# Every second transfer of expert weights begun from ScalarE's queue

## The chip, the cores and the metric

The kernel runs on 1 core of one Trainium2 chip. The metric is the device time of one execution, in microseconds (us).

## The reference

One sequence of 512 tokens, model width 1024, float32, passes through two blocks. The first mixes a gated linear attention with a gated convolution and adds a gated embedding; the second mixes an mLSTM branch with a differential attention and ends in an expert layer. Only that layer is touched by the change:

```python
def expert_choice_ffn(h, w_router, w_gate, w_up, w_down):
    cap = EC_CAPACITY * S // N_EXPERTS            # 2 * 512 // 16 = 64 tokens for an expert
    aff = jax.nn.softmax(jnp.einsum('bsd,de->bse', h, w_router), axis=-1)
    g, idx = lax.top_k(aff.transpose(0, 2, 1), cap)
    xe = h[bidx, idx]
    hid = (jax.nn.silu(jnp.einsum('becd,edf->becf', xe, w_gate))
           * jnp.einsum('becd,edf->becf', xe, w_up))
    ye = jnp.einsum('becf,efd->becd', hid, w_down) * g[..., None]
    return jnp.zeros_like(h).at[bidx, idx].add(ye)
```

There are 16 experts of width 2048. `w_gate` and `w_up` are 1024 x 2048 for each and `w_down` is 2048 x 1024: 24 MB of weights for an expert, 384 MB in all, each read once.

## The kernel before

The dense part comes first (up to about 1,109 us into the span): 168 tiles of weights of 512 KB each go through six slots. Then tokens are routed, and the expert loop runs (from 1,140 us to 2,077 us), with a short final norm and the store behind it.

**Chunks and the ring.** An expert's weights come as `PER = 24` chunks of 1 MB: n = 0 to 7 are gate rows, 8 to 15 up rows, 16 to 23 down rows. Chunks are numbered on over all experts, g = 24e + n, from 0 to 383. A ring of `RING = 18` slots holds them: 12 in the tensor `ring_a`, 6 in `ring_b`, chunk g in slot g mod 18. A gate or up chunk is one row of 8 KB for each of the 128 partitions; a down chunk is two rows of 4 KB for each.

**Who loads.** SyncE (SP) begins every transfer of weights, in order of g. The first 18 chunks are fetched while the dense part and the routing run, as their places become free. From g = 18 on, `load_expert` (L603 to L610) waits until the count `s_used` has reached g - 17, that is, until TensorE has finished chunk g - 18, and issues the transfer. A transfer adds 16 to the semaphore of its slot when it has landed.

**TensorE (PE)** works one expert after the other, in an order written out by hand: gate chunk 0; `placed` (L2085), the 8 products that put the previous expert's output back to the tokens; gate 1 to 7 and up 0 to 7 (`gate_up`, L2102); `gather` for the next expert (L2063); `hidden_turned` (L2122) and `gather_turned` (L2070); down 0 to 5 (`down`, L2113); `place_turned` (L2080); down 6 and 7. Each chunk begins with a wait for its slot's semaphore, and its last product adds 1 to `s_used`. In the last expert a product of the residual (L2126) stands behind each down chunk but the last.

**ScalarE (ACT)** runs, for each expert: wait for `used(e, 7)` (gate chunk 7 done); two Silu activations of the gate result (L1076); `gathered(e + 1)`, a copy of the gathered tokens (L1070); the copy `hidT0` (L1080); the copy `place` after `place_turned` (L1082); wait for `used(e, 23)`; the copy `ye` of the expert's output (L1086), for which `placed(e)` waits. It begins no transfer here; its only three are small ones at the very start.

**VectorE** multiplies the two halves of the hidden layer, scales the gathered tokens and adds the placed results; GpSimd does nothing in this loop.

Of the kernel before, what the change touches and what calls it, by code (L numbers as in the profile page):

```python
# [34 lines left out]
NE, CAP, FF = 16, 64, 2048  # L35
BIG = 3.0e38
KB = 1024
RING, RING_A = 18, 12
PER = 24
# [117 lines left out]
STREAM, TILES = dense_stream()  # L157
AT = {(gr.name, gr.i): gr.g for gr in STREAM}
FIRST = [min(gr.g for gr in STREAM if n in gr.tiles) for n in range(len(TILES))]
# [67 lines left out]
def kernel_program(nc, xT_in, pT_in, table, gla_mask_in, rstm_in, negm_in, selr_in, m01_in, dist_in, tiles_in,  # L227
                   w_gk2, diff_lam_2, w_router_2, w_gate_e_2, w_up_e_2, w_down_e_2, norm_f_g_2, x3_store, out):
    ctx = ExitStack()
    with ctx:  # L230
# [10 lines left out]
        def sem(name):  # L241
            return ctx.enter_context(nc.semaphore(name))
# [286 lines left out]
        s_ring = [sem(f"ring_in{s}") for s in range(RING)]  # L529
        s_used = sem("ring_used")  # L530
# [27 lines left out]
        gate_v = w_gate_e_2[0].rearrange("e (k p) f -> p e k f", p=P)  # L558
        up_v = w_up_e_2[0].rearrange("e (k p) f -> p e k f", p=P)
        down_v = w_down_e_2[0].rearrange("e (c j p) d -> p e c j d", p=P, j=2)  # L560

        def used(eng, e, n):
            eng.wait_ge(s_used, e * PER + n + 1)

        def slot(e, n):
            s = (e * PER + n) % RING
            return ring_a[:, s, :] if s < RING_A else ring_b[:, s - RING_A, :]

        def last_pair(t):

            return ps[:, (0, 2, 6, 4)[t]:(0, 2, 6, 4)[t] + 2, :]
# [13 lines left out]
        def stage_done(eng, name, i):  # L585
            eng.wait_ge(t_mm, AT[name, i] + 1)
# [7 lines left out]
        @block.sync  # L594
        def _(sp):

            def load1(n):
                if n >= SLOTS:
                    sp.wait_ge(t_mm, LAST[n - SLOTS] + 1)
                src = tiles_in[n].rearrange("p (k c) -> p k c", c=P)  # L600
                sp.dma_start(d_raw[:, n % SLOTS, :, :], src).then_inc(t_raw[n % SLOTS], 16)

            def load_expert(e, first=0, last=PER):  # L603
                for n in range(first, last):
                    g = e * PER + n
                    src = gate_v[:, e, n, :] if n < 8 else up_v[:, e, n - 8, :] if n < 16 else down_v[:, e, n - 16, :, :]
                    dst = slot(e, n) if n < 16 else slot(e, n).rearrange("p (j d) -> p j d", j=2)
                    if g >= RING:
                        sp.wait_ge(s_used, g - RING + 1)
                    sp.dma_start(dst, src).then_inc(s_ring[g % RING], 16)  # L610

            load1(0)
            for n in range(4):
                sp.dma_start(x_in[:, 2 * n:2 * n + 2, :], xT_in[:, 2 * n:2 * n + 2, :]).then_inc(s_xk[n], 16)
            for n in range(1, len(TILES)):
                if FIRST[n] == AT["za", 0]:
                    sp.dma_start(gla_mask[:, :, :], gla_mask_in[:, :, :]).then_inc(s_mask, 16)
                    sp.dma_start(m01[:, :, :], m01_in[:, :, :]).then_inc(s_m01, 16)
                elif FIRST[n] == AT["xc", 4]:
                    sp.wait_ge(lo_dve.sem, lo_dve.count("lo1", TT - 1))  # L620
                    sp.dma_start(x1[:, :, :], xT_in[:, :, :]).then_inc(s_x1, 16)
                elif FIRST[n] == AT["out", 6]:
                    stage_done(sp, "yc", 7)
                    sp.dma_start(pT_raw[:, :, :], pT_in[:, :, :]).then_inc(s_p, 16)
                elif FIRST[n] == AT["gate", 5]:
                    stage_done(sp, "out", 7)
                    sp.dma_start(rstm[:, :], rstm_in[:, :]).then_inc(s_rows, 16)
                    sp.dma_start(negm[:, :], negm_in[:, :]).then_inc(s_rows, 16)
                    sp.dma_start(selr[:, :, :], selr_in[:, :, :]).then_inc(s_rows, 16)
                elif FIRST[n] == AT["dv", 0] and TILES[n][3] == 0:  # L630
                    sp.wait_ge(r_dve.sem, r_dve.count("mb"))
                    sp.dma_start(alibi[:, :], dist_in[:, :]).then_inc(s_dist, 16)
                elif FIRST[n] == AT["mo", 0]:
                    sp.wait_ge(x3_pool.sem, x3_pool.count(f"x{KD - 1}"))
                    sp.dma_start(x3_store[:, :, :], x1[:, :, :]).then_inc(s_spill, 16)
                elif FIRST[n] == AT["mo", 2]:
                    sp.wait_ge(s_spill, 16)
                    sp.dma_start(lam_sb[:, :, :], diff_lam_2[0].rearrange("a c -> (a c)").partition_broadcast(P)).then_inc(s_lam, 16)
                elif FIRST[n] == AT["ub", 0]:
                    stage_done(sp, "ua", 7)  # L640
                    sp.dma_start(xT[:, :, :], x3_store[:, :, :]).then_inc(s_x3, 16)
                    sp.dma_start(rw[:, :, :], w_router_2[0].rearrange("(k p) e -> p k e", p=P)).then_inc(s_rw, 16)
                elif STREAM[FIRST[n]].name == "out2" and STREAM[FIRST[n]].i < 5:
                    if STREAM[FIRST[n]].i == 0:
                        sp.wait_ge(do_lo.sem, do_lo.count("lo", NH - 1))
                    load_expert(0, STREAM[FIRST[n]].i, STREAM[FIRST[n]].i + 1)
                load1(n)
            sp.wait_ge(mb_dve.sem, mb_dve.count("lo", 7))
            load_expert(0, 5, RING_A)
            stage_done(sp, "out2", 7)  # L650
            load_expert(0, first=RING_A)
            for e in range(1, NE):
                load_expert(e)
            used(sp, NE - 1, 15)
            sp.dma_start(gbc[:, :], norm_f_g_2.partition_broadcast(P)).then_inc(s_g, 16)
            for t in range(TT):
                sp.wait_ge(z_dve.sem, z_dve.count(f"y{t}"))
                sp.dma_start(out[0, t * P:(t + 1) * P, :], fin[:, t, :]).then_inc(s_store[t % 2], 16)
            for t in range(2):
                sp.wait_ge(s_store[t], 32)  # L660
# [67 lines left out]
        def _(act):  # L728
# [339 lines left out]
            def gathered(e):  # L1068
                act.wait_ge(x_pe.sem, x_pe.count("gather", e))
                x_act.done(act.activation(xg[:, :], ps[:, 5, :], ACT.Copy), "xg")  # L1070

            gathered(0)
            for e in range(NE):
                used(act, e, 7)
                for q in range(2):
                    e_act.done(act.activation(sg[:, q, :], ps[:, q, :], ACT.Silu), f"s{q}")  # L1076
                if e + 1 < NE:
                    gathered(e + 1)
                act.wait_ge(e_pe.sem, e_pe.count("hT", e))
                e_act.done(act.activation(hidT[:, 0, :, :], ps[:, 6, :], ACT.Copy), "hT0")  # L1080
                act.wait_ge(e_pe.sem, e_pe.count("place", e))
                e_act.done(act.activation(place[:, :], ps[:, 5, :], ACT.Copy), "place")  # L1082
                if e == NE - 1:
                    z_act.done(act.activation(esm[:, 40:41], eps[:, :], ACT.Sqrt), "warm")
                used(act, e, 23)
                e_act.done(act.activation(ye[:, :], ps[:, 4, :], ACT.Copy), "ye")  # L1086
            for t in range(TT):
                act.wait_ge(e_pe.sem, e_pe.count(f"o{t}", NE - 1))
                if t:
                    act.wait_ge(z_act.sem, z_act.count(f"root{t - 1}"))  # L1090
                z_act.done(act.activation(zsq[:, :].rearrange("p (d c) -> p d c", d=2), last_pair(t), ACT.Square,
                                          accum_out=esm[:, 16 + t:17 + t]), f"ss{t}")
                act.wait_ge(z_act.sem, z_act.count(f"ss{t}"))
                z_act.done(act.activation(esm[:, 20 + t:21 + t], esm[:, 16 + t:17 + t], ACT.Sqrt, bias=eps[:, :], scale=1 / D),
                           f"root{t}")
# [1164 lines left out]
```

## Time and profile before

| what | us |
|---|---|
| three timed runs: median (lowest to highest) | 2097.74 (2092.34 to 2097.86) |
| the profiled execution, its own time | 2091.48 |
| span of its profile, first to last instruction | 2089.4 |
| TensorE busy, share of the span | 1934.3, 93% |
| VectorE, ScalarE busy | 725.9, 523.4 |
| mean granted clock of TensorE | 0.990 of full speed |

The profile names engines PE (TensorE's matmuls), PEld (its weight loads), DVE (VectorE), ACT, POOL and SP; SPq and ACTq are the sequencers of SP and ACT, on which transfers are issued. DMA share is the mean busy share of the core's 16 DMA engines; it can read slightly over 1, since the records of packets overlap a little.

### The profile page before, as it was taken

The numbers are of one execution on the slowest core, as the hardware profiler recorded it, in microseconds if no ns is written. First come the engines' busy times: TensorE is split into PE (matmuls) and PEld (weight loads), VectorE is DVE, ScalarE is ACT, GpSimd is POOL, SyncE is SP. The second block draws the span as 40 slices with busy tenths as digits, with TensorE's granted clock in tenths as the row PEclk, the third lists the DMA queues.
The fourth block names the chain that finished last, engine by engine and source line by source line (L and its number), as shares of the span: only waits on it lengthen the run. The fifth ranks groups of instructions, "written<-read, shape, count | busy, mean of one in ns | idle before, by whom it ended". The sixth has DMA issues, their size and how long they took to land.

```text
span 2089.4 us, 20846 instructions
## 1 busy us (share of the span) xinstructions
PE 1934.3 (93%) x8754; PEld 1146.5 (55%) x8754; DVE 725.9 (35%) x1121; ACT 523.4 (25%) x816; POOL 80.5 (4%) x67
## 2 busy tenths in 40 slices
PE   7999999999999899899986999988888898888897
PEld 6777788888877777677863333322222232222232
DVE  6534544333456775666443111101111111011111
ACT  4443422322245442456622000000000000000001
POOL 2000000000014401000000000000000000000000
PEclk9999999999999999999998999999999999999999
DMA  4221133233323222212554999999999999999996
GB/s 164 89 91 51 61 131 101 93 100 100 103 81 111 91 80 73 91 61 65 193 217 159 419 418 416 417 416 416 418 419 419 416 416 417 417 417 419 418 417 276
DMA packets 100012, 505.37 MB, mean 242 GB/s; under 512 B 10240, under 2 KB 10752, under 8 KB 66768
## 3 DMA queue, kind: packets, MB, share of 16 engines
q1 hardware_dynamic: 99600, 503.88, 61.4%
q8 instruction: 69, 1.13, 0.2%
q10 hardware_dynamic: 320, 0.17, 0.0%
q14 instruction: 23, 0.19, 0.0%
HBM read 499.82 MB, written 4.19 MB: 241 GB/s over the span
## 4 chain that ended last, share of the span: by engine, by line
PE 62%; DMA 28%; DVE 4%; ACT 3%; SPq 1%; issue 1%; POOL 1%; ACTq 0%; DVEq 0%; POOLq 0%
PE ps L1784 37%; DMA ring_a<-in_w_up_e 10%; PE ps L2102 9%; DMA ring_a<-in_w_gate_e 7%; DMA ring_b<-in_w_up_e 6%; DMA ring_b<-in_w_gate_e 4%; PE ps L2113 3%; PE ps L1743 3%; PE ps L2085 2%; SPq L610 1%; PE ps L2063 1%; PE ps L1958 1%; PE ps L1835 1%; PE ps L1832 1%; PE ps L1934 1%
## 5 line engine op out<-in xcount | busy, mean ns | idle before, releaser
L2102 PE MATMUL ps<-ring_a,xe 128*64 128x512 f32 x1376 | 318.2, 599 | 50.6 <-DMA ring_a<-in_w_up_e 35.2
L1102 DVE TENSOR_TENSOR d_lo<-d_raw,d_hi 128x1024 fp32r<-128x1024 f32 x168 | 210.6, 1263 | 113.8 <-ACT d_hi L735 113.3
L2102 PEld LDWEIGHTS ps<-ring_a,xe 128*64 128x64 f32 x1376 | 90.9, 136 | 275.4 <-issue 165.2
L2102 PE MATMUL ps<-ring_b,xe 128*64 128x512 f32 x672 | 156.8, 600 | 28.2 <-DMA ring_b<-in_w_up_e 20.4
L1291 DVE TENSOR_TENSOR hid<-sg,ps 128x512 f32<-128x512 f32 x32 | 20.6, 684 | 466.2 <-PE ps L2102 466.2
L1784 PE MATMUL ps<-n_hi,d_hi 128*128 128x512 f32 x448 | 175.6, 392 | 1.5 <-DVE d_lo L1102 0.8
L735 ACT ACTIVATE d_hi<-d_raw 128x1024 fp32r<-128x1024 f32 x168 | 173.0, 1049 | 10.2 <-DMA d_raw<-in_tiles_in 9.5
L1784 PE MATMUL ps<-n_hi,d_lo 128*128 128x512 f32 x448 | 174.5, 389 | 0.0
L1784 PE MATMUL ps<-n_lo,d_hi 128*128 128x512 f32 x448 | 174.4, 389 | 0.0
L1665 DVE TENSOR_TENSOR x<-x,ps 128x1024 f32<-128x1024 f32 x60 | 69.2, 1215 | 271.6 <-PE ps L2085 271.6
L2113 PE MATMUL ps<-ring_a,hidT 128*64 128x512 f32 x688 | 156.1, 597 | 6.1 <-ACT hidT L1080 3.9
L2102 PEld LDWEIGHTS ps<-ring_b,xe 128*64 128x64 f32 x672 | 44.0, 136 | 139.7 <-issue 77.5
L1784 PE MATMUL ps<-h_hi,d_hi 128*128 128x512 f32 x256 | 104.1, 407 | 9.3 <-DVE d_lo L1102 9.3
L2113 PEld LDWEIGHTS ps<-ring_a,hidT 128*64 128x64 f32 x688 | 53.1, 137 | 93.9 <-issue 76.6
L1784 PE MATMUL ps<-h_lo,d_hi 128*128 128x512 f32 x256 | 101.1, 395 | 0.0
L1784 PE MATMUL ps<-h_hi,d_lo 128*128 128x512 f32 x256 | 100.9, 394 | 0.0
L1784 PEld LDWEIGHTS ps<-n_hi,d_hi 128*128 128x128 f32 x448 | 84.1, 188 | 20.1 <-issue 1.7
L1784 PEld LDWEIGHTS ps<-n_hi,d_lo 128*128 128x128 f32 x448 | 84.1, 188 | 17.6
L1784 PEld LDWEIGHTS ps<-n_lo,d_hi 128*128 128x128 f32 x448 | 84.1, 188 | 17.0
L1076 ACT ACTIVATE sg<-ps 128x512 f32<-128x512 f32 x32 | 17.4, 594 | 299.3 <-PE ps L2102 299.3
L1070 ACT ACTIVATE xg<-ps 128x512 f32<-128x512 f32 x16 | 9.6, 598 | 327.3 <-PE ps L2063 327.3
L2113 PE MATMUL ps<-ring_b,hidT 128*64 128x512 f32 x336 | 76.6, 597 | 3.5 <-ACT hidT L1080 2.4
(421 smaller groups left out, 2684.3 us busy)
## 6 DMA issues: line engine op xcount, KB each, us to landing
ring_a<-in_w_gate_e SPq DMA_DIRECT2D x88, 1024.0 KB, 20.9
ring_a<-in_w_down_e SPq DMA_DIRECT2D x86, 1024.0 KB, 23.2
d_raw<-in_tiles_in SPq DMA_DIRECT2D x168, 512.0 KB, 3.4
ring_a<-in_w_up_e SPq DMA_DIRECT2D x84, 1024.0 KB, 27.1
ring_b<-in_w_up_e SPq DMA_DIRECT2D x44, 1024.0 KB, 27.0
ring_b<-in_w_down_e SPq DMA_DIRECT2D x42, 1024.0 KB, 23.3
ring_b<-in_w_gate_e SPq DMA_DIRECT2D x40, 1024.0 KB, 21.1
x_in<-in_xT_in SPq DMA_DIRECT2D x4, 512.0 KB, 6.6
```

The costliest lines, as they stand in the source:

```text
L610: sp.dma_start(dst, src).then_inc(s_ring[g % RING], 16)
L735: act.activation(d_hi[:, n % SLOTS, :, :], d_raw[:, n % SLOTS, :, :], ACT.Copy).then_inc(t_hi, 1)
L1102: dve.tensor_tensor(d_lo[:, n % SLOTS, :, :], d_raw[:, n % SLOTS, :, :], d_hi[:, n % SLOTS, :, :].bitcast(F32), ALU.subtract).then_inc(t_l ...
L1665: e_dve.done(dve.tensor_tensor(row, row, ps[:, b:b + 2, :], ALU.add), f"o{t}")
L1743: mm = pe.matmul(bank, lt[:, k, t * P:(t + 1) * P], rhs, start=k == 0 and m == 0, stop=k == KD - 1 and m == 2)
L1784: mm = pe.matmul(bank, lt[:, n, gr.k0 + k, :], rt[:, k, :], start=k == 0 and m == 0, stop=k == gr.nk - 1 and m == 2)
L1832: pe.matmul(ps[half, 2 + h // 2, h % 2 * GDV:(h % 2 + 1) * GDV], qT[:, h, tokc], state[:, h, :], start=False, stop=c == 1, skip_group_chec ...
L1835: mm = pe.matmul(ps[:, 4 + h // 2, h % 2 * GDV:(h % 2 + 1) * GDV], kd_tok[half, i, h * GDK:(h + 1) * GDK], v_tok[half, i, h * GDV:(h + 1) ...
L1934: mm = pe.matmul(ps[:, 5 + h % 2, q * P:(q + 1) * P], aaT[:, n % 2, c, :], d_tok[:, c, h * DDV:(h + 1) * DDV], start=c == 0, stop=c == TT - 1)
L2085: return pe.matmul(ps[:, bank, :], place[half, t * P:(t + 1) * P], ye[half, :], start=start, stop=True, skip_group_check=True)
L2102: mm = pe.matmul(ps[half * CAP:(half + 1) * CAP, 2 * m + q, :], xe[:, k, :], slot(e, n)[:, (2 * q + half) * S:(2 * q + half + 1) * S], sta ...
L2113: mm = pe.matmul(ps[d * CAP:(d + 1) * CAP, 4, :], hidT[:, q, c, half * CAP:(half + 1) * CAP], slot(e, n)[:, j * D + d * S:j * D + (d + 1) ...
```

## The change

Chunks up to g = 17 are loaded as before. From g = 18 on, SP issues the even chunks only, in order. The odd chunks (19, 21, ... 383) are issued by ACT on its own DMA queue, in three places of its loop: after the two Silu of expert e, those that fill the slots of n = 0 to 7; after the copy `place`, those for n = 8 to 15; after the copy `ye`, those for n = 16 to 23. In numbers of chunks: 24e + 19, 21, 23, 25 after the Silu; 24e + 27, 29, 31, 33 after `place`; 24e + 35, 37, 39, 41 after `ye`. Each issue carries the same wait on `s_used` as before; at those places it is already met.

```diff
+        def load_slot(queue, g):
+            e, n = divmod(g, PER)
+            src = gate_v[:, e, n, :] if n < 8 else up_v[:, e, n - 8, :] if n < 16 else down_v[:, e, n - 16, :, :]
+            dst = slot(e, n) if n < 16 else slot(e, n).rearrange("p (j d) -> p j d", j=2)
+            if g >= RING:
+                queue.wait_ge(s_used, g - RING + 1)
+            queue.dma_start(dst, src).then_inc(s_ring[g % RING], 16)
...
-            load_expert(0, first=RING_A)
-            for e in range(1, NE):
-                load_expert(e)
+            load_weights(RING_A, RING)
+            load_weights(RING, NE * PER, 2)
...
+            def load_others(e, n, least):
+
+                for g in range(max(RING + 1, e * PER + least + RING) | 1, min(e * PER + n + RING + 1, NE * PER), 2):
+                    load_slot(act, g)
+
             gathered(0)
             for e in range(NE):
                 used(act, e, 7)
                 for q in range(2):
                     e_act.done(act.activation(sg[:, q, :], ps[:, q, :], ACT.Silu), f"s{q}")
+                load_others(e, 7, 0)
...
                 e_act.done(act.activation(place[:, :], ps[:, 5, :], ACT.Copy), "place")
+                load_others(e, 15, 8)
...
                 e_act.done(act.activation(ye[:, :], ps[:, 4, :], ACT.Copy), "ye")
+                load_others(e, 23, 16)
```

`load_weights(first, last, step)` on SP calls `load_slot(sp, g)` for each g of that range.

## Rows read from the trace of the kernel before

**Rows 1.** The page: data rate in 40 equal slices, and the queues

```profile
GB/s 164 89 91 51 61 131 101 93 100 100 103 81 111 91 80 73 91 61 65 193 217 159 419 418 416 417 416 416 418 419 419 416 416 417 417 417 419 418 417 276
...
q1 hardware_dynamic: 99600, 503.88, 61.4%
q10 hardware_dynamic: 320, 0.17, 0.0%
```

**Rows 2.** Busy time by stretch: us, then each engine (count), PE clock, DMA share, GB/s

```profile
1142.00:1193.00 51.00, 50.61 (x242) 18.46 (x238) 4.75 (x6) 3.48 (x6) 0.00 (x0) 1.00 0.98 401
1193.00:1244.00 51.00, 50.60 (x242) 18.52 (x240) 8.05 (x12) 3.48 (x6) 0.00 (x0) 1.00 1.02 416
...
1348.00:1408.00 60.00, 53.13 (x240) 17.37 (x238) 8.23 (x11) 3.48 (x6) 0.00 (x0) 1.00 1.02 418
```

**Rows 3.** Timeline of ACT in experts 0 and 1

```profile
1154.34 1.09 ACT L1076 ACTIVATE sg<-ps 128x512 f32<-128x512 f32 x2 [14.26 <-PE ps L2102]
1171.50 0.60 ACT L1070 ACTIVATE xg<-ps 128x512 f32<-128x512 f32 x1 [16.08 <-PE ps L2063]
...
1184.46 0.60 ACT L1082 ACTIVATE place<-ps 128x512 f32<-128x512 f32 x1 [11.34 <-PE ps L2080]
1188.05 0.60 ACT L1086 ACTIVATE ye<-ps 128x512 f32<-128x512 f32 x1 [3.00 <-PE ps L2113]
1205.57 1.09 ACT L1076 ACTIVATE sg<-ps 128x512 f32<-128x512 f32 x2 [16.92 <-PE ps L2102]
```

**Rows 4.** The chain that ended last: start, length, what

```profile
1295.48 26.37 DMA ring_b<-in_w_up_e
...
1477.70 26.38 DMA ring_b<-in_w_up_e
...
1537.93 26.37 DMA ring_a<-in_w_up_e
...
2022.67 26.39 DMA ring_b<-in_w_up_e
```

**Rows 5.** Busy time by stretch, two stretches of 5 us of the stream

```profile
1655.00:1660.00 5.00, 4.64 (x24) 1.45 (x22) 1.44 (x4) 0.00 (x0) 0.00 (x0) 1.00 1.03 424
...
1690.00:1695.00 5.00, 4.61 (x28) 2.32 (x26) 1.29 (x2) 1.20 (x2) 0.00 (x0) 1.00 1.02 408
```

**Rows 6.** Timeline of PE at the end of the last expert

```profile
2049.11 1.94 PE L2102 MATMUL ps<-ring_b,xe 128*64 128x512 f32 x8 [0.58 <-DMA ring_b<-in_w_up_e]
...
2054.42 1.94 PE L2113 MATMUL ps<-ring_b,hidT 128*64 128x512 f32 x8 [0.39 <-ACT hidT L1080]
...
2057.35 1.94 PE L2113 MATMUL ps<-ring_b,hidT 128*64 128x512 f32 x8
...
2074.89 1.94 PE L2113 MATMUL ps<-ring_a,hidT 128*64 128x512 f32 x8
```

**Rows 7.** The last two issues of weights (chunks 382, 383), and their time to landing

```profile
L610 SPq DMA_DIRECT2D ring_a<-in_w_down_e x2: 2345/2360/2374, 2048.8 to 2051.2; - x2
...
DMA to landing us min/median/max: 18.1/18.2/18.2
```

**Rows 8.** SP's issues from 1629 to 1641 us: min/median/max duration in ns

```profile
L610 SPq DMA_DIRECT2D ring_a<-in_w_gate_e x8: 433/1158/3147, 1629.0 to 1640.0; - x8
```

**Rows 9.** SP's issue of chunk 18: duration of the issue, time to landing

```profile
L610 SPq DMA_DIRECT2D ring_a<-in_w_down_e x1: 368/368/368, 1142.3 to 1142.3; - x1
...
DMA to landing us min/median/max: 5.2/5.2/5.2
```

**Rows 10.** Timeline of SP: first and last issues of expert 0's window

```profile
1142.31 8.95 SPq L610 DMA_DIRECT2D ring_a<-in_w_down_e  x6
...
1186.33 14.81 SPq L610 DMA_DIRECT2D ring_a<-in_w_down_e  x6
```

**Rows 11.** Timeline of PE in expert 0 and into expert 1

```profile
1173.31 3.65 PE L2113 MATMUL ps<-ring_b,hidT 128*64 128x512 f32 x16 [0.39 <-ACT hidT L1080]
...
1193.29 8.80 PE L2102 MATMUL ps<-ring_a,xe 128*64 128x512 f32 x40
```

More of the change, by code:

```diff
@@ L601, in load1, with load_weights @@
                 sp.dma_start(d_raw[:, n % SLOTS, :, :], src).then_inc(t_raw[n % SLOTS], 16)
[L603 to L610, printed above, removed]
+            def load_weights(first, last, step=1):
+                for g in range(first, last, step):
+                    load_slot(sp, g)
             load1(0)
@@ L645, in _ @@
                         sp.wait_ge(do_lo.sem, do_lo.count("lo", NH - 1))
-                    load_expert(0, STREAM[FIRST[n]].i, STREAM[FIRST[n]].i + 1)
+                    load_weights(STREAM[FIRST[n]].i, STREAM[FIRST[n]].i + 1)
                 load1(n)
             sp.wait_ge(mb_dve.sem, mb_dve.count("lo", 7))
-            load_expert(0, 5, RING_A)
+            load_weights(5, RING_A)
             stage_done(sp, "out2", 7)
-            load_expert(0, first=RING_A)
-            for e in range(1, NE):
-                load_expert(e)
+            load_weights(RING_A, RING)
+            load_weights(RING, NE * PER, 2)
             used(sp, NE - 1, 15)
```

## The prediction

> **What bounds the kernel now.** I read the page's row of data rates first [rows 1]: low and changing up to the 22nd of 40 slices, then 416 to 419 GB/s to the last but one. So the 922 us from about 1,142 to 2,064 us, the expert loop, are one unbroken stream of weights, nearly all on one hardware queue (503.88 MB). The busy time by stretch says who sets the pace there [rows 2]: in the second stretch PE is busy 50.60 of 51 us, and in the last one 53.13 of 60 us, with the DMA share at 1.02 in both. PE alone needs 51.2 us for an expert (the Silu of expert 0 starts at 1154.34, that of expert 1 at 1205.57 [rows 3]). The engines need more: the chain that ended last reaches PE's first wait for a chunk at 1295.48 and then repeats every 60.2 us (1477.70, 1537.93) to the last expert [rows 4]. 24 chunks in 60.2 us are 2.51 us for a chunk on average; at 408 and 424 GB/s, the slow and fast stretches [rows 5], one MB takes 2.57 us (down chunks, rows of 4 KB) or about 2.48 us. The early experts look bound by PE, but they only use up the 18 chunks fetched ahead, and the engines never pause after the first start: [rows 2] show 416 GB/s while PE is still the busier. A pause of the engines anywhere after 1,142 us thus moves the end by its own length, and so does a change of their rate.
>
> The end is the one place where that chain is left. The last up chunk (375) releases PE at 2049.11 [rows 6]; then come the turned hidden layer and eight down chunks with a residual product each, one every 2.93 us (2054.42 to 2057.35), slower than the 2.57 us of a transfer. The last chunk lands at 2051.2 + 18.2 = 2069.4 [rows 7], PE reads it only at 2074.89. So what counts at the end is when chunk 375 lands, not 383.
>
> **The change, part by part.**
>
> *Issue cost.* SP gives up 183 issues and ACT takes them: 12 for each expert. SP had nothing to gain: it is far ahead, 18 us from issue to landing even at the end [rows 7], and its issues of 433 to 3147 ns [rows 8] are long because its queue is full, as against 368 ns with an empty one [rows 9]. Worth 0. On ACT four issues cost 4 x 0.37 = 1.5 us, or 4 x 1.16 = 4.6 us at the median of the full queue [rows 8]. After the Silu the next work, `xg`, comes 16 us later, after `ye` the next Silu 17 us later: hidden. After `place`, `ye` is due 3.0 us later [rows 3]: 1.5 us are hidden, 4.6 us would make `ye` and with it `placed` 1.6 us late. PE has 60.2 - 51.2 = 9 us of waiting in each expert to absorb that. I take 0; the other bound is 1.6 us in each of the two or three experts before PE waits, and these too lie beside the stream, so it stays near 0.
>
> *The start.* Before, SP issues a chunk every 1.72 us from 1142.31, as PE frees slots ((8.95 - 0.37) / 5 [rows 10]), faster than the engines move one: no pause. Now only even chunks come, every 3.43 us, until ACT gets to its first four. The time from issue to first byte is the same for all, so I put each transfer at its issue. Chunks 18, 20, 22 fill 1142.3 to 1144.9, 1145.7 to 1148.3, 1149.2 to 1151.8, chunk 24 fills 1152.6 to 1155.1, and ACT's 19 starts when the two Silu are done, 1155.4 [rows 3]. Pauses: 0.8 + 0.9 + 0.8 + 0.3 = 2.8 us. Then 19, 21, 23, 25 and SP's 26, 28, 30, 32 are 20.2 us of work, to 1175.7, when 34 has been freed by the first down chunk (1173.31 + 1.9 [rows 11]). 34 ends at 1178.2; 36 comes at 1178.7, 38 at 1182.1 and ends at 1184.6; the next four of ACT come after `place`, at 1185.1 [rows 3]. Pauses: 0.5 + 0.9 + 0.5 = 1.9 us. From there twelve chunks or so are always open. Sum: **4.7 us**. If the issue costs more or the engines' uneven finish hides part of the pauses, 3 to 7 us.
>
> *The order.* At 1184.6 the even chunks are in through 38, the odd ones through 25: the evens lead by 13 numbers, 6.5 chunks. From then on both queues hold work, and I assume that the engines serve them equally, an odd chunk every 5.0 us. Chunk 27 (issued 1185.1, in by about 1192.7) is in time for PE, which starts gate 3 at 1193.29 + 2 x 1.72 = 1196.7 [rows 11]; 29 and 31 are in at 1197.7 and 1202.7 for 1200.2 and 1203.6; 33 comes at 1207.7 for 1207.0, and now PE goes at the pace of the odd queue. Nothing brings the odds forward: SP stops only when it is 17 numbers ahead of PE, and the odd queue gets the full rate only then. It costs nothing in the middle, since the engines are busy all the time. It does in the last expert: when chunk 375 lands, evens that PE needs later are already in. Before, 8 chunks came after it; now all evens are through (382 when the odds are at about 369) and only 377, 379, 381, 383 come after it. It lands 4 x 2.57 = **10.3 us** later in the stream. The tail behind is the same, since one transfer every 2.57 us still outruns PE's 2.93. If the lead were L chunks less than 4, this term would be 2.5 L, at least about 2.5 us, because 375 and its even neighbour then land together.
>
> *Sum.* 4.7 + 10.3 = 15.0 us on the profiled execution's 2091.48: 2106.5, or 0.72%. The median of the timed runs stands 6.3 us above that execution, so 15 us on 2097.74 makes 2112.7; I say **2112 us**.
>
> **Is ACT late in steady state?** When chunk 21 of an expert has been used, ACT's queue holds 23 and 25, 5.1 us at full rate, 10 us at half; the next four come after `place_turned` and `place` (0.7 + 0.6 us and the first byte's 2.6 us, 5.2 minus 2.57 [rows 9]): 3.9 us. Tight only if SP's queue is empty at that moment. After up 7 PE spends some 8 us on `gather` and the turns, in which no slot is freed; with a lead near 6.5 seven chunks (17.7 us) are still open then, and SP gets three more before ACT's turn at about 20 us. No pause, with about 3 us to spare.
>
> **The rivals.**
>
> A. *The order is kept.* If the engines took the two queues nearly by time of issue, or the evens were held back otherwise, only the start and one shared pair are left: 4.7 + 2.5 = 7 us, 2105 us. For it: in-order service of one queue. Against: nothing in the trace orders two queues.
>
> B. *Two queues move more (the other side: not slower).* The engines may leave a little time between packets of one queue that a second fills; the gap of 408 to 424 GB/s between 4 KB and 8 KB rows [rows 5] shows that there is a cost for each packet. 1% more rate is 9.2 us of the 922. If all went at 424 instead of 417, 1.7%, that gives 15 us back: 2097 us, no change. It decides from 1.0% (less than 0.3% slower) and makes the kernel faster from 2.3%, 427 GB/s, which no row shows; 3% would give 2097.7 + 15 - 27.6 = 2085. Against: the share is already 1.02. The Trainium skill, DMA: Bandwidth & Descriptors, section Issuing engines are not separate DMA queues, says that transfers begun on several engines run on the same 16 DMA engines and interleave, and that only issue time is saved. By it this rival gains nothing; no row here has two loaded queues to test it, while the share of 1.02 agrees with it.
>
> C. *ACT comes late in every expert.* If the lead reaches its limit of 8.5, one chunk (2.5 us) of pause in each of 15 experts: 15 + 37 = 52 us at most, half of it likelier, 2135 to 2150 us. The margin of 3 us above speaks against it.
>
> D. *Two queues move less.* 1% less rate from switching between them: 15 + 9 = 24 us, 2122 us. No row for or against; mirror of B.
>
> **Chances.** Forecast 0.45, A 0.15, B 0.20, C 0.10, D 0.10. No change is within 0.3%, 6.3 us, which is about what a measurement of this kernel can tell from nothing. Faster comes from B alone, 0.14; within 0.3%: 0.06 of B, 0.08 of A, 0.05 of the low end of the forecast: 0.19; slower 0.67. The forecast's own range is 3 + 5 to 7 + 12 us, 2106 to 2117. The range for 8 in 10 takes in A and D and the part of B up to a gain of 2%: 2092 to 2126.
>
> **What the profile after would show.** A data rate by stretch below 400 GB/s between 1,142 and 1,190 us (before: 401 with the first start in it), about 380, and 416 to 419 after it; a rate of 424 would be B, repeated dips C. PE's first wait for a chunk near 1,207 us instead of 1,295, on odd chunks only, one every 5 us where it was 2.5. Chunk 375 landing near 2,064 and PE's last down chunk near 2,090. ACT's issues short after `place`, `ye` on time. The median from issue to landing should be far longer for ACT's transfers than for SP's at the moment PE needs them. I would be wrong if the evens' lead did not last (A), or if the rate changed (B, D).

## The result, and the profile after

| | before | after |
|---|---|---|
| timed runs, median of 5 | 2094.61 us | 2108.02 us (2106.32 to 2112.67) |
| ratio, with its 95% interval | 1 | 1.0066 (1.0048 to 1.0083) |
| profiled execution, its own time | 2091.48 | 2109.94 |
| span of its profile | 2089.4 | 2106.7 |

The change makes the kernel 0.66% slower, 13.4 us by the medians and 14 by the ratio. The forecast was 15 us and 0.72%, 2112 us.

The page of the changed kernel, the data rate in 40 equal slices and the queues, for [rows 1]; q10 is ACT's queue:

```profile
GB/s 164 97 80 58 53 140 92 98 100 93 107 93 98 80 103 70 77 63 103 179 180 189 399 418 417 416 417 417 417 418 418 417 418 416 417 417 417 418 417 205
...
q1 hardware_dynamic: 65184, 311.98, 38.9%
q10 hardware_dynamic: 34736, 192.07, 22.3%
```

183 chunks, 191.9 MB, have moved to ACT's queue, and the rate in the loop is the same to 1 or 2 GB/s. Two loaded queues carry 417 GB/s, as one does: rivals B and D are out. The Trainium skill, DMA: Bandwidth & Descriptors, section Issuing engines are not separate DMA queues, says that a second issuing engine saves issue time alone; this trace with two loaded queues agrees. Inside the loop only the 23rd slice is lower, 399 for 419.

In this execution chunk 18 is issued at 1145.41 instead of 1142.31. That looks like no effect of the change: all runs below have it between 1145.1 and 1146.5, the one with SP alone too, and the profiled execution of the kernel before was 3.1 us below its median. So I count from that issue. Busy time by stretch of the changed kernel, from there on and much later, for [rows 2]:

```profile
1145.00:1196.00 51.00, 50.60 (x242) 18.46 (x238) 4.65 (x6) 3.47 (x6) 0.00 (x0) 1.00 0.94 358
1196.00:1247.00 51.00, 46.40 (x216) 16.13 (x214) 6.21 (x10) 2.88 (x5) 0.00 (x0) 0.97 1.02 418
1547.00:1607.00 60.00, 53.51 (x240) 17.83 (x238) 8.28 (x11) 2.94 (x6) 0.00 (x0) 0.95 1.02 417
```

The first stretch moves 358 instead of 401 GB/s: (401 - 358) x 51 / 417 = 5.3 us of pauses. After it there are none.

The chain that ended last, for [rows 4]:

```profile
1509.39 39.72 DMA ring_a<-in_w_down_e
...
1569.62 39.75 DMA ring_a<-in_w_down_e
...
2036.93 29.47 DMA ring_b<-in_w_up_e
```

The period is still 60.2 us, but what PE waits for has changed from up chunks to down chunks, and a transfer on the chain takes 39.7 us from issue to landing instead of 26.4. The last line is chunk 375: 2036.93 + 29.47 = 2066.40, that is 921.0 us after the issue of chunk 18. Before it was 2022.67 + 26.39 = 2049.06 [rows 4], less 1142.3: 906.8. The whole 14.2 us lie there; the tail behind it is 40.3 us in both (2106.7 - 2066.4 and 2089.4 - 2049.1).

ACT's timeline in expert 0, for [rows 3]:

```profile
1157.43 0.60 ACT L1083 ACTIVATE sg<-ps 128x512 f32<-128x512 f32 x1 [14.27 <-PE ps L2112]
1157.44 0.92 ACTq L575 DMA_DIRECT2D ring_a<-in_w_down_e  x2
1157.92 0.59 ACT L1083 ACTIVATE sg<-ps 128x512 f32<-128x512 f32 x1
...
1187.55 0.60 ACT L1090 ACTIVATE place<-ps 128x512 f32<-128x512 f32 x1 [11.34 <-PE ps L2090]
1187.56 0.83 ACTq L575 DMA_DIRECT2D ring_a<-in_w_gate_e  x2
...
1191.14 0.60 ACT L1095 ACTIVATE ye<-ps 128x512 f32<-128x512 f32 x1 [3.00 <-PE ps L2123]
```

The issues after `place` end at 1189.8, 1.4 us before `ye`, which waits 3.00 us for PE as before. Issue costs nothing here.

### The profile page after: what moved, and what is told of

Same layout as the page of the kernel before. It is cut to its first block, busy times and chain, and to the rows that moved or that the text cites. A ratio compares the mean times of both kernels' runs of the same rounds, so it can differ in the third digit from the quotient of the medians.

```text
span 2106.7 us, 20846 instructions
## 1 busy us (share of the span) xinstructions
PE 1947.0 (92%) x8754; PEld 1152.4 (55%) x8754; DVE 726.7 (34%) x1121; ACT 523.5 (25%) x816; POOL 81.5 (4%) x67
## 4 chain that ended last, share of the span: by engine, by line
PE 33%; DMA 29%; DVE 3%; ACT 2%; issue 1%; ACTq 0%; DVEq 0%
DMA ring_a<-in_w_down_e 17%; PE ps L1794 12%; PE ps L2112 10%; DMA ring_b<-in_w_down_e 9%; PE ps L2123 3%; PE ps L2095 2%; DMA ring_a<-in_w_gate_e 2%; PE ps L1753 2%; DMA ring_b<-in_w_up_e 1%; PE ps L1968 1%; PE ps L1944 1%; PE ps L2073 0%; PE ps L1889 0%; PE ps L2136 0%; PE ps L1955 0%
## 5 line engine op out<-in xcount | busy, mean ns | idle before, releaser
L2112 PE MATMUL ps<-ring_a,xe 128*64 128x512 f32 x1376 | 308.5, 596 | 6.7 <-DMA ring_a<-in_w_up_e 3.0
L2123 PE MATMUL ps<-ring_a,hidT 128*64 128x512 f32 x688 | 173.9, 643 | 51.2 <-DMA ring_a<-in_w_down_e 47.3
L2112 PE MATMUL ps<-ring_b,xe 128*64 128x512 f32 x672 | 151.6, 596 | 4.2 <-DMA ring_b<-in_w_up_e 3.0
L2123 PE MATMUL ps<-ring_b,hidT 128*64 128x512 f32 x336 | 84.4, 635 | 32.0 <-DMA ring_b<-in_w_down_e 29.6
## 6 DMA issues: line engine op xcount, KB each, us to landing
ring_a<-in_w_gate_e SPq DMA_DIRECT2D x48, 1024.0 KB, 22.5
```

Source lines behind the costliest of these rows:

```text
L2112: mm = pe.matmul(ps[half * CAP:(half + 1) * CAP, 2 * m + q, :], xe[:, k, :], slot(e, n)[:, (2 * q + half) * S:(2 * q + half + 1) * S], sta ...
L2123: mm = pe.matmul(ps[d * CAP:(d + 1) * CAP, 4, :], hidT[:, q, c, half * CAP:(half + 1) * CAP], slot(e, n)[:, j * D + d * S:j * D + (d + 1) ...
```

## The experiments

All times are medians, and each ratio is against runs of the kernel before on the same chip. Those had medians of 2094.61 us beside the changed kernel, 2093.46 beside start_sp, end_sp and both_sp, and 2094.09 beside the last four, so a difference in us between two rows of the table that were not run together can be off by 1 us or so. For each run I also read from its trace three moments: the issue of chunk 18, the landing of 375 and the landing of the last chunk, 383 (us). Counted from the issue of chunk 18 to the end of the span, each run's difference from before lies within the interval of its ratio, and the moments say in which part of the loop the time is lost.

| kernel | us | ratio (interval) | 375 in, from the issue of 18 | 383 in | chunks that land after 375 |
|---|---|---|---|---|---|
| before | 2094.61 | 1 | 906.8 | 927.1 | 8 |
| after | 2108.02 | 1.0066 (1.0048 to 1.0083) | 921.0 | 933.7 | 5 |
| start_sp | 2102.18 | 1.0041 (1.0028 to 1.0054) | 915.0 | 929.0 | 6 |
| end_sp | 2100.38 | 1.0033 (1.0021 to 1.0044) | 911.5 | 931.7 | 8 |
| both_sp | 2095.03 | 1.0006 (0.9997 to 1.0015) | 906.6 | 926.8 | 8 |
| rows8k_one | 2084.87 | 0.9951 (0.9938 to 0.9963) | 898.4 | 918.2 | 8 |
| rows8k_two | 2103.40 | 1.0044 (1.0031 to 1.0056) | 913.2 | 924.3 | 4 |
| early_b | 2103.18 | 1.0043 (1.0030 to 1.0055) | 916.4 | 932.5 | 6 |
| late_b | 2119.31 | 1.0126 (1.0109 to 1.0144) | 932.1 | 943.3 | 4 |

**start_sp: the pauses alone taken away.** SP loads every chunk through 42.

```diff
-            load_weights(RING, NE * PER, 2)
+            load_weights(RING, 43)
+            load_weights(44, NE * PER, 2)
...
-                for g in range(max(RING + 1, e * PER + least + RING) | 1, ...
+                for g in range(max(43, e * PER + least + RING) | 1, ...
```

> SP loads every chunk through 42, ACT begins with chunk 43 after the Silu of expert 1. Theory (the loss is pauses of the DMA engines in expert 0, about 5 us in the changed kernel, plus 7 to 8 us because chunk 375 lands in a changed order): the pauses go, the order stays. The data rate of the first 51 us after chunk 18 is issued is 400 GB/s or more instead of 334, and the time is 5 us below the changed kernel, about 8 to 9 us above before. Rival 1 (the loss is spread over the whole loop, a little in each expert, through two queues or ACT's lateness): only one of 16 experts is relieved, 1 us below the changed kernel, 12 to 13 us above before. Rival 2 (the evens' lead is made only by the pauses of expert 0 and lasts because nothing brings the odds forward): the order term goes too, no more than 3 us above before.

Measured: 5.8 us below the changed kernel, 0.41% above before. The first stretch, from 1145 us:

```profile
1145.00:1196.00 51.00, 50.61 (x242) 18.37 (x238) 4.94 (x7) 3.47 (x6) 0.00 (x0) 1.00 0.99 402
```

The rate is that of before (401), so the pauses are gone, and they cost 5 to 6 us. "Spread over the loop" would have left all but 1 us. The second rival falls too, and tells something on the lead of the evens: by how many numbers they are ahead when an odd chunk lands. There is none while SP loads alone; it is 5 numbers at n = 1 of expert 2 and 9 at n = 3, and 9 at its widest from there on (11 in the changed kernel). The step from 5 to 9 comes while ACT's queue is empty: the trace has no packet of it (q10) from 1237.0 to 1242.0 us, between ACT's first two turns, and SP's queue never stops in that expert. After that ACT's queue stands still for no more than 0.3 us at a time. In the changed kernel it stands still once too, for 7.7 us in expert 0. So the lead does not need pauses of the engines. It is made in the first expert that ACT loads, and then nothing brings the odds forward.

**end_sp: the order alone restored.** ACT's last chunk is 353, and SP issues 354 to 383 in order.

```diff
-            load_weights(RING, NE * PER, 2)
+            load_weights(RING, 355, 2)
+            load_weights(355, NE * PER)
...
-... min(e * PER + n + RING + 1, NE * PER), 2):
+... min(e * PER + n + RING + 1, 355), 2):
```

> ACT's last chunk is 353 (expert 14), and SP loads 354 to 383 in order. Theory: the order at chunk 375 is that of before, so 375 lands 8 chunks before the last again; the pauses of expert 0 stay. About 7 us below the changed kernel, 6 to 7 us above before. Rival (spread over the loop): two of 16 experts relieved, 1 to 2 us below the changed kernel. Rival (order has no price, all is in the start): the time of the changed kernel.

Measured: 7.6 us below the changed kernel, 0.33% above before. Relief of two experts of 16 would have given 1 to 2 us, and no price of the order none, so both rivals fall. 8 chunks land after 375 again. The last chunk lands at 931.7, still 4.6 us later than before, which is the size of the pauses.

**both_sp: both edits together** (ACT issues 43 to 353, the odd ones).

> ACT issues odd chunks from 43 to 353 only; SP issues all others. Theory: both terms are gone, 0 to 2 us above before, although 156 of the 183 issues still come from ACT and PE still waits for odd down chunks at a lower clock in every expert. Rival (spread over the loop): 10 to 12 us above before.

Measured: 1.0006 (0.9997 to 1.0015), no difference from before, and chunk 375 lands 0.2 us earlier. The stretch in the middle, in the kernel before and in both_sp:

```profile
1547.00:1607.00 60.00, 53.49 (x240) 17.55 (x240) 8.28 (x11) 3.27 (x7) 0.00 (x0) 1.00 1.02 417
...
1547.00:1607.00 60.00, 54.48 (x240) 17.81 (x238) 8.04 (x11) 3.47 (x6) 0.00 (x0) 0.94 1.02 417
```

So 156 issues from ACT, the new place of PE's waits and the lower clock (0.94 in this stretch, 1.00 before) cost nothing that this measurement can tell. With the other two this makes a table of two by two, in the landing of 375: the pauses cost 4.9 us (911.5 - 906.6) without the order's term and 6.0 (921.0 - 915.0) with it, the order 8.4 (915.0 - 906.6) and 9.5 (921.0 - 911.5).

**rows8k_two and rows8k_one: packets of one size.** A down chunk is read as rows of 8 KB; the transposes of the hidden layer take their columns to match, so that the result stays the same.

```diff
-        down_v = w_down_e_2[0].rearrange("e (c j p) d -> p e c j d", p=P, j=2)
+        down_v = w_down_e_2[0].rearrange("e (c p j) d -> p e c (j d)", p=P, j=2)
...
-  hid[:, q, c * P:(c + 1) * P]
+  hid[:, q, c // 2 * 2 * P + c % 2:(c // 2 + 1) * 2 * P:2]
```

> The changed kernel with the same down rows of 8 KB, so that all chunks have packets of one size. Theory P (the engines take packets in turn from the two queues, so that 4 KB packets get a third of the bytes beside 8 KB ones): odd down chunks, which land 7.2 us apart in the changed kernel, land 5.0 us apart, the evens' lead stays at about one value over an expert instead of swinging between 5 and 11 numbers. The order term then comes to 4 chunks, 10 us: about 15 us above the one-queue kernel with these rows, 6 to 7 us above before. Theory Q (the turns go by bytes or by whole transfers, and the 7.2 us have another cause, such as ACT's late issue): the spacing stays near 7 us.

The three odd down chunks 91, 93 and 95 are issued within a microsecond; their times to landing show how far apart they come. The changed kernel, and then rows8k_two:

```profile
L575 ACTq DMA_DIRECT2D ring_a<-in_w_down_e x3: 385/482/2182, 1326.2 to 1327.2; - x3
...
DMA to landing us min/median/max: 26.2/33.0/39.7
```

```profile
L575 ACTq DMA_DIRECT2D ring_a<-in_w_down_e x3: 335/444/453, 1324.9 to 1325.8; - x3
...
DMA to landing us min/median/max: 28.4/33.0/37.5
```

In the changed kernel they land (39.7 - 26.2 + 0.95) / 2 = 7.2 us apart, in rows8k_two (37.5 - 28.4 + 0.86) / 2 = 5.0 us. That is theory P. A packet in these records is one row. While the even queue is already at gate chunks, with packets of 8 KB, and the odd one still at down chunks, with 4 KB, equal turns by packets give the odd ones a third of the bytes. The packets in the traces show it directly: from 1344 to 1362 us ACT's queue starts 639 packets, all of 4 KB, and SP's 598, all of 8 KB; in rows8k_two it is 461 and 466, all of 8 KB. When the evens are in down chunks and the odds in up chunks it is two thirds, and the odds come 3.8 us apart. So the lead swings between 11 and 5 numbers in the changed kernel; with one packet size it stays at 9 from n = 1 to n = 15.

In the last expert 4 chunks land after 375 then, as I had forecast for the changed kernel itself: rows8k_two is 14.8 us behind rows8k_one at chunk 375 (913.2 - 898.4). At the end it is more than the 15 us expected. From the issue of chunk 18 to the end of the span it is 16.0 us, since the part behind 375 has grown from 40.4 to 41.6 us: chunk 373 comes so late there that PE is not done with it when 375 lands. By the medians it is 18.5 us, and 9.3 us above before, where 6 to 7 were expected. Of the rest 1.4 us lies ahead of chunk 18 in the two profiles.

> The kernel before (SP alone), but a down chunk is read as rows of 8 KB: each partition gets two neighbouring rows of w_down instead of two that stand 128 rows apart, and the transposes of the hidden layer take every second column to match. The result is the reference's. Down chunks then move as fast as gate and up chunks: 2.49 instead of 2.56 us. From chunk 24 to 375 there are 14 times 8 down chunks, 112 x 0.07 = 8 us: about 8 to 9 us below before. If the cost of 4 KB rows is not in the packets, no change. If the strided read of the transposes costs, it is in PE's slack, 0.

Measured: 0.9951, 9 to 10 us below before. The data rate in its page:

```profile
GB/s 165 91 89 51 60 132 101 91 102 92 110 81 103 89 90 74 91 61 61 173 224 140 416 421 421 421 421 421 421 422 421 421 422 421 421 422 421 421 421 272
```

It is 421 GB/s instead of 417 throughout the loop, and chunk 375 lands 8.4 us earlier. This kernel is faster than the one before and the changed one.

**early_b: ACT's second turn 11 us earlier**, right after the copy `hidT0`.

```diff
                 e_act.done(act.activation(hidT[:, 0, :, :], ps[:, 6, :], ACT.Copy), "hT0")
+                load_others(e, 15, 8)
...
                 e_act.done(act.activation(place[:, :], ps[:, 5, :], ACT.Copy), "place")
-                load_others(e, 15, 8)
```

> The changed kernel, but ACT issues the four chunks that fill the slots of n = 8 to 15 right after the copy hidT0 instead of after place, 11 us earlier; their slots are free by then. Theory: the odd queue has work at 1172.5 instead of 1185.1, so the later pauses of expert 0 (1.9 us) go. The evens' lead grows only where the odd queue is empty, so it starts near 3.5 chunks instead of 6.5 and the order term shrinks by 2 to 5 us. Together 4 to 7 us below the changed kernel, 7 to 10 above before. If the lead comes from the packet sizes alone, only the 1.9 us.

Measured: 4.8 us below the changed kernel, 375 lands 4.5 us earlier, and the lead swings between 7 and 3 numbers instead of 11 and 5. ACT's queue, which stood still for 7.7 us in expert 0, no longer stops at all. The last chunk lands only 1.2 us earlier, so most of the gain is order: ACT's late second turn is worth 4 of the 11 numbers. The other 7 are there with a queue that never runs empty; ACT's first turn still comes 12 us after SP has begun.

**late_b: the same turn later**, after `ye`.

```diff
-                load_others(e, 15, 8)
...
                 e_act.done(act.activation(ye[:, :], ps[:, 4, :], ACT.Copy), "ye")
+                load_others(e, 15, 8)
                 load_others(e, 23, 16)
```

> The changed kernel, but ACT issues the four chunks that fill the slots of n = 8 to 15 only after ye, together with the next four: 3.6 to 5 us later. It asks how wide the margin is that I put at 3 us. Theory: the first pauses grow by 2 to 3 us (SP's chunk 40 at 1186.3 fills a part), and in later experts the queues stay full or nearly so: 2 to 6 us above the changed kernel. Rival C (no margin left in each expert): 2 to 4 us of pause in each of 15 experts, 30 to 60 us above, and a data rate of 400 GB/s or less throughout instead of 417.

Measured: 11.3 us above the changed kernel, between the 2 to 6 and the 30 to 60 us expected. Two neighbouring stretches of 5 us, before and at ACT's turn:

```profile
1550.00:1555.00 5.00, 4.49 (x16) 1.29 (x12) 0.00 (x0) 0.60 (x1) 0.00 (x0) 0.71 1.03 424
1555.00:1560.00 5.00, 4.85 (x22) 1.75 (x24) 0.09 (x1) 0.60 (x1) 0.00 (x0) 1.00 0.96 354
```

The second has a pause of some 0.8 us (354 of 417), as have others of the turns: the last chunk lands 9.6 us later than in the changed kernel, 0.6 us for each of the 16 experts on average. A delay of 3.6 to 5 us thus uses up the margin, which I had put at 3 us, and a little more; the changed kernel itself is inside it.

## Why the prediction was right

**What bounds it.** Held. The period is 60.2 us before and after, the rate 417 GB/s, and the pauses of expert 0 show at the end, 4.6 us in end_sp.

**Issue cost, 0.** Held: `ye` of expert 0 waits for PE as long as before, and both_sp, with 156 issues on ACT, has no loss.

**The start, 4.7 us.** Held. The first stretch says 5.3 us, the last landing of end_sp 4.6, the two by two 4.9 to 6.0. ACT's first issue came 1 us earlier than I had it, with the first Silu and not behind the second. The rate that I named for this stretch, about 380 GB/s, did not fit my own sum, which asks for some 360; measured were 358.

**The order, 10.3 us.** The mechanism is right: end_sp gives it back, and the evens' lead is made in expert 0, where ACT's queue is empty, and lasts to the end. I had it at a constant 13 numbers; it swings between 11 and 5. The term's size in the changed kernel is 7.6 us by the landings, the time from 375 to the last landing being 12.7 us (933.7 - 921.0) instead of 20.3 (927.1 - 906.8). The mis-sized step is "I assume that the engines serve them equally": they do by packets, not by bytes, and at chunk 375, with evens already in down chunks, the lead is 5 numbers, so chunk 382 is still open and 5 chunks come after 375 instead of 4. The assumption also misplaced PE's first wait. I had it at chunk 33, at 1207 us, which is 1210 counted from the later issue of chunk 18. But PE was on time for all gate and up chunks of expert 1 and first waited for down chunk 45. This is PE's timeline there:

```profile
1227.64 8.80 PE L2123 MATMUL ps<-ring_a,hidT 128*64 128x512 f32 x40 [0.39 <-ACT hidT L1088]
1239.34 3.40 PE L2123 MATMUL ps<-ring_a,hidT 128*64 128x512 f32 x8 [2.90 <-DMA ring_a<-in_w_down_e]
...
1246.50 1.94 PE L2123 MATMUL ps<-ring_a,hidT 128*64 128x512 f32 x8 [1.31 <-DMA ring_a<-in_w_down_e]
```

**The sum.** 5.0 us of pauses (the first engine to finish chunk 383 is that much later, 925.7 for 920.7 us), 7.6 of order, and 1.6 us by which the slowest of the 16 engines finishes further behind the first (8.0 instead of 6.4 us): 14.2. The last term I had not foreseen. It is seen where ACT loads to the end (8.2 us in start_sp, 7.6 in early_b) and not where SP does (6.8 in end_sp, 6.5 in both_sp), and with it the order comes to 9.2 us, as the table of two by two has it, 8.4 to 9.5. But late_b, where ACT loads to the end as well, has 2.2 us. What makes it is not settled. So the nearness of 15.0 and 14.2 is partly luck: the order was 2.7 us too large for the lead, and 1.6 us of another kind were missing.

**The rivals.** A (order kept) fell with 5 instead of 8 chunks after 375; B and D with the rate of 417; C with no pause after the first stretch, though late_b shows it one step away. Whatever the outcome, 0.14 for a faster kernel was too much: it needed 427 GB/s or more, which no row showed.

**A sign that failed.** I expected far longer times from issue to landing for ACT's transfers than for SP's. Median us from issue to landing stand last in these lines of the changed kernel's page:

```profile
ring_a<-in_w_gate_e SPq DMA_DIRECT2D x48, 1024.0 KB, 22.5
ring_a<-in_w_down_e SPq DMA_DIRECT2D x43, 1024.0 KB, 20.0
ring_a<-in_w_down_e ACTq DMA_DIRECT2D x43, 1024.0 KB, 33.0
ring_a<-in_w_gate_e ACTq DMA_DIRECT2D x40, 1024.0 KB, 18.0
```

It is so for down chunks, 33.0 against 20.0, and the other way for gate chunks, 18.0 against 22.5: ACT issues those late, when only two to four transfers are open in its queue.

## What to carry to other kernels

In the kernel before, the DMA engines never paused in the loop after its start, and a second queue added no data (417 GB/s with one and with two); it took away the order in which the data came. Before splitting such a stream, look at the engine that will issue. ACT's turns are tied to late points of its own work, so its queue ran empty once, at the start, its half fell behind and stayed behind, and the price was paid in two places: pauses at the start, and at the end, where the last transfer that PE needs lands later. What helped here was the length of the rows: 8 KB instead of 4 KB gave 0.5%.

## What the runs showed of the hardware that I had not expected

**Two queues take turns by packets.** Chunks of 4 KB packets beside ones of 8 KB land 7.2 us apart, 5.0 us with equal packets, and the queues start about as many packets each (639 and 598). The Trainium skill, DMA: Bandwidth & Descriptors, section Queues, rings and completion order, says that each engine goes round between its queues packet by packet. The spacings and counts agree with it in that turns go by count and not by bytes; how many rows make one turn, they do not tell.

**ACT issues a transfer while its activation runs.** The activation `place` starts at 1187.55, the issue written behind it at 1187.56, 0.59 us before its end.

**TensorE's clock was lower after a long wait for data.** The timeline of PE in the changed kernel, and the clock (the column before the DMA share) in two stretches around that wait:

```profile
1352.52 3.65 PE L2123 MATMUL ps<-ring_a,hidT 128*64 128x512 f32 x16 [0.79 <-DMA ring_a<-in_w_down_e]
1359.74 3.68 PE L2123 MATMUL ps<-ring_a,hidT 128*64 128x512 f32 x8 [3.57 <-DMA ring_a<-in_w_down_e]
```

```profile
1353.00:1356.00 3.00, 3.00 (x16) 0.86 (x12) 0.00 (x0) 0.00 (x0) 0.00 (x0) 1.00 1.03 422
...
1359.00:1362.00 3.00, 2.26 (x6) 0.77 (x8) 0.00 (x0) 0.00 (x0) 0.00 (x0) 0.50 1.02 418
```

After the wait of 3.57 us the granted clock is 0.50, 1.2 GHz, and 8 products take 3.68 instead of 1.94 us. The wait of 2.90 us before chunk 45, shown above, is followed by 3.40 us, the one of 1.31 us by 1.94. The mean over the span falls from 0.990 to 0.976; in rows8k_two, where odd and even chunks come 5.0 us a pair and PE's longest wait for a chunk is 2.2 us, it is 0.988. Here PE's slack covers it; in a kernel bound by PE such a wait would cost some 1.7 us more than its own length, an estimate from 3.68 - 1.94.

**A queue with much open work holds the issue.** The fourth issue of ACT after the Silu takes 6.7 us where the others take 0.4 to 2.2. This is ACT's timeline at the end of expert 2 and in expert 3:

```profile
1310.05 0.45 ACTq L575 DMA_DIRECT2D ring_b<-in_w_down_e  x1
...
1327.18 2.18 ACTq L575 DMA_DIRECT2D ring_a<-in_w_down_e  x1
1329.40 6.72 ACTq L575 DMA_DIRECT2D ring_a<-in_w_gate_e  x1
1344.55 0.60 ACT L1072 ACTIVATE xg<-ps 128x512 f32<-128x512 f32 x1 [17.25 <-PE ps L2073]
```

At that moment seven of ACT's transfers are open, four of them down chunks. It is not their number alone: at 1310.05 us, with eight open and none of them a down chunk, an issue took 0.45 us. A down chunk has twice the packets, so a limit by packets would fit, but no run tests it. ACT's next work is due 8 us after the issue ends, so nothing is late; placed right before an activation that PE waits for, such an issue could hold up PE, which was not tried.
